# First mixer: the last two pooled projections and two modulation slices come ahead of the last gate projection

## What is computed

```python
u = h @ w_in                                   # 768 x 3072
a = u[..., :CONV_W] * jax.nn.sigmoid(u[..., CONV_W:2 * CONV_W])
bp = u[..., 2 * CONV_W:]
a = dwconv(a, w_dw, b_dw, pad)                 # 31 taps, each channel by itself
a = jax.nn.silu(layernorm(a, ln_g, ln_b))
pooled = jnp.stack([centred_mean(bp[..., g, :], w) - bp[..., g, :]
                    for g, w in enumerate(POOL_WINDOWS)], axis=-2)
p = jnp.einsum('...gc,gcd->...gd', pooled, w_pool) + b_pool
return jnp.concatenate([a, p], axis=-1) @ w_out
...
mod_lat = jnp.split((sc @ w_ada[l] + b_ada[l])[:, None, :], 6, axis=-1)
```

## Time and profile before

| what | value |
|---|---|
| median of three runs | 2460.28 us |
| the profiled execution | 2461.31 us, span 2459.7 us |
| TensorE matmuls busy | 2321.2 us, 94% of the span |
| VectorE busy | 1625.6 us, 66% |
| ScalarE busy | 946.8 us, 38% |
| GpSimd busy | 427.6 us, 17% |
| share of TensorE in the chain that ended last | 81% (DMA 9%, VectorE 4%) |
| mean DMA rate | 264 GB/s |

### The profile page before, as it was taken

One profiled execution on the slowest core, in us unless ns is written; L12 is line 12 of the kernel. 1 busy time (PEld: TensorE's weight loads), 2 busy tenths in 40 slices (PEclk: granted clock), 3 DMA queues, 4 the chain that ended last, 5 costly groups with the idle time before them and its releaser, 6 DMA issues.

```text
span 2459.7 us, 42712 instructions
## 1 busy us (share of the span) xinstructions
PE 2321.2 (94%) x16387; PEld 1553.2 (63%) x16388; DVE 1625.6 (66%) x2005; ACT 946.8 (38%) x1167; POOL 427.6 (17%) x461
## 2 busy tenths in 40 slices
PE   6999989999999999999969999999999899999984
PEld 3555534457888888888847887666644455555542
DVE  2899985447898889888976651677534633454544
ACT  3000014115777777777754232466421111111111
POOL 0633431220000000000020000211000223233323
PEclk8999989999999999999989999999999899999997
DMA  9111075539999999999992132212543979999997
GB/s 342 58 44 59 34 293 167 182 113 402 421 401 388 380 395 383 385 389 392 378 380 81 62 124 104 87 54 75 193 154 140 412 313 376 404 421 420 420 420 309
DMA packets 154320, 649.12 MB, mean 264 GB/s; under 512 B 27866, under 2 KB 42874, under 8 KB 99458
## 3 DMA queue, kind: packets, MB, share of 16 engines
q1 hardware_dynamic: 126624, 577.40, 59.7%
q0 software_dynamic: 16192, 57.53, 6.5%
q10 hardware_dynamic: 11426, 13.12, 1.5%
HBM read 595.13 MB, written 52.86 MB: 263 GB/s over the span
## 4 chain that ended last, share of the span: by engine, by line
PE 81%; DMA 9%; DVE 4%; ACT 2%; issue 2%; POOL 1%; SPq 0%; ACTq 0%; DVEq 0%; POOLq 0%
PE ps L970 78%; DMA arena<-in_w_dram 6%; DMA chunk<-in_w_ada_dram 1%; ACT arena L1616 1%; DVE arena L2380 1%; PE ps L1212 1%; PE ps L1190 1%; PE ps L1196 1%; DMA arena<-h_d,uix 1%; PE ps L1059 1%; POOL arena L769 0%; DMA buf_d<-arena 0%; PE ps L1586 0%; DMA arena<-in_w_ada_dram 0%; DMA arena<-buf_d,slots 0%
## 5 line engine op out<-in xcount | busy, mean ns | idle before, releaser
L970 PE MATMUL ps<-arena 128*32 128x256 f32 (+5 forms) x10296 | 1188.7, 407 | 38.9 <-DVE arena L2380 12.3
L970 PEld LDWEIGHTS ps<-arena 128*32 128x32 f32 (+1 forms) x10296 | 652.5, 129 | 521.1 <-issue 318.5
L2433 DVE TENSOR_TENSOR wl<-wx,wh 128x2048 fp32r<-128x2048 f32 x228 | 511.1, 2285 | 18.5 <-ACT wh L1616 18.5
L1616 ACT ACTIVATE arena<-ps 128x256 f32<-128x256 f32 (+5 forms) x389 | 176.4, 478 | 864.0 <-PE ps L970 616.9
L1616 ACT ACTIVATE wh<-wx 128x2048 fp32r<-128x2048 f32 x228 | 432.4, 1915 | 80.8 <-PE ps L970 75.9
L2380 DVE COPY arena<-arena 128x2048 f32<-128x2048 f32 x180 | 222.7, 1297 | 273.1 <-PE ps L970 228.8
L970 PE MATMUL ps<-wh,xT 128*128 128x512 f32 x1184 | 379.2, 394 | 1.2 <-issue 0.7
L970 PEld LDWEIGHTS ps<-wh,xT 128*128 128x128 f32 x1184 | 222.5, 188 | 53.1 <-issue 1.2
L2502 DVE SCALAR_TENSOR_TENSOR arena<-arena,par 128x768 f32<-128x768 f32 x232 | 241.1, 1112 | 0.0
L970 PE MATMUL ps<-wl,xT 128*128 128x512 f32 x608 | 239.4, 394 | 0.0
L970 PE MATMUL ps<-wh,gT 128*128 128x512 f32 x608 | 199.5, 399 | 0.0
(11 more groups left out here) (362 smaller groups left out, 2267.1 us busy)
## 6 DMA issues: line engine op xcount, KB each, us to landing
wx<-in_w_dram SPq DMA_DIRECT2D x228, 1024.0 KB, 8.4
arena<-in_w_dram SPq DMA_DIRECT2D x192, 1024.0 KB, 21.8
arena<-in_w_ada_dram SPq DMA_DIRECT2D x40, 1024.0 KB, 8.6
craw<-in_w_in_c_dram SPq DMA_DIRECT2D x8, 2048.0 KB, 8.7
buf_d<-arena POOLq DMA_DIRECT2D x1, 14848.0 KB, 57.5
arena<-buf_d POOLq DMA_DIRECT2D x19, 512.0 KB, 10.0
buf_d<-arena POOLq DMA_DIRECT2D x19, 512.0 KB, 7.7
arena<-in_w_in_ab_dram SPq DMA_DIRECT2D x8, 1024.0 KB, 12.6
```

What stands on the lines that cost most here:

```text
L970: return pe.matmul(bank_ap, lhsT, rhs, start=first, stop=last)
L1616: return act.activation(out_, in_, f, **kw)
L2433: v.tensor_tensor(wl[:, g], wx[:, g], whs[g % NH].bitcast(F32), ALU.subtract).then_inc(m["low"], 1)
```

## The change

Only the table of steps is written in another order; loads, buffers, waits inside the steps and all arithmetic stay.

```diff
-for _step in ("V0 G0 P0 V1 G1 P1 V2 G2 P2 V3 p0 G3 P3 V4 p1 G4 P4 V5 G5 P5 V6 p2 G6 p3 V7 P6 G7 p4 P7 "
-              "s0 s1 p5 s2 s3 s4 s5 s6 p6 s7 s8 s9 p7 s10 s11").split():
+for _step in ("V0 G0 P0 V1 G1 P1 V2 G2 P2 V3 p0 G3 P3 V4 p1 G4 P4 V5 G5 P5 V6 p2 G6 p3 P6 V7 P7 s0 s1 G7 "
+              "p4 s2 s3 s4 s5 p5 p6 s6 s7 s8 p7 s9 s10 s11").split():
```

## The result

The changed kernel takes 2464.54 us, the median of 20 runs; the kernel before takes 2460.66 us, the median of 20 runs beside it. The medians lie 3.9 us apart. The ratio is 1.0019 with a 95% interval of 1.0012 to 1.0027, that is 4.7 us (3.0 to 6.6). So the changed kernel is slower: a small loss, by either figure inside the 0.2% that had been called no change, though the upper end of the interval is not. Two of its 20 runs stand apart, 2486.80 and 3494.04 us, at mean granted clocks of 0.95 and 0.63 where the others have 0.97; the second is left out of the ratio, and without both the median is 2464.50 us. The time lies 0.8 us above the predicted 2463.7, and 0.4 of these because the kernel before takes 2460.66 us in the 20 runs and not 2460.28. The profiled execution took 2462.43 us.

The account below looks back on a forecast made before the run. The end of s11 was taken to bound the stage, VectorE next. 2461.31 + 3.4 = 2464.7 us for an execution like the profiled one, which lies 1.03 above the median, so 2463.7 us predicted; range 2459.0 to 2468.5.

Parts of the forecast that it names:

- The limit: End of the stage: set by the end of s11, at 348.43 us before, with VectorE 1.73 us behind as next limit.
- The late gate: G7 ends 13.4 us later, at 310.7; VectorE takes tile 7's product at 322.63, hidden with 11 us to spare.
- The longer wait: SyncE waits for all gates until 310.7, not 297.28; both panels go together, s4 starts at 326.5, TensorE idles 11 us.
- `s4` and `s5`: Slices 4 and 5 on TensorE after the idle: the same 4.45 us as before, ending at 331.0.
- `p5` and `p6`: Projections now ahead of s6: full speed, 2.85 us each; s6 ends at 338.8, 10 us later.
- The wait for GpSimd: TensorE's 3.20 us wait ahead of p6 for GpSimd's tile 7: gone.
- The tail: Loads of s9 to s11, released behind s6 to s8: three left instead of two, s11 ends at 351.8, 3.4 us later.
- VectorE: Convolutions beside GpSimd's pooling: end moves by 0 to 4.2 us, to 361.1 at most, covered by second sums at 362.0.
- Cold projections: Rival: p5 and p6 at half clock, 5.46 us each; +6.0 us with one, +8.6 with both; chance 0.29.
- The full queue: Rival: loads overlap, transfers bound, s11 ends at 346.8; 2458.7 us, or up to 2461.3 with partial overlap; chance 0.15.

Follow-up runs that it names:

- extra load: The changed kernel with one more transfer of 1.25 MB, used by nobody, ahead of the first panel: 2467.95 us.
- panel behind: The changed kernel with SyncE issuing the P-step panel behind P7, then s4's load, and only the gate panel after the wait for G7: 2460.52 us.
- its version with fill: The changed kernel with SyncE's panels reordered, plus six output-projection filler steps instead of four ahead of the wait for the last convolution: 2457.86 us.
- release sooner: The changed kernel with slice n loaded when slice n-4 is done, not n-3, using a fourth load semaphore: 2459.76 us.
- Each half of the change alone: Two kernels: the changed order up to G7 and p4 with the old rest, 2460.41 us; the old order up to s1 with the new rest, 2459.55 us.

## Why the prediction was right

*The limit* was the end of `s11`, and VectorE next: shown from both sides, by the extra load (one to one to the end) and by the panel behind (TensorE at once waits for VectorE).

Times in this section are set on the axis of the kernel before, 1.28 us later than in the rows above. *The late gate* ended at 311.4 for the forecast 310.7, and hid behind VectorE, which took its sigmoid 15 us later. *The longer wait*: the panels left together, `s4` started at 327.3 for 326.5, idle 11.52 for 11. *`s4` and `s5`* took 4.0 us, up to the start of `p5`, instead of 4.45. *`p5` and `p6`* ran at full speed, 2.85 us each, with 1.08 us between them. *The wait for GpSimd* is gone.

*The tail* is the term that was off in size: from the release of `s9` to the end of `s11` I had 13.0 us (338.8 to 351.8); it took 11.6 (339.2 to 350.8), mainly because the three loads landed 2.5 to 2.6 us apart and not 3.4 and 3.2. The 3.4 came from one pair of transfers; the 2.7 us per MB of the same prediction would have been nearer. So `s11` ended 2.3 us later than 348.43, not 3.4. Another 0.6 us, which the sum did not have, was lost in the first sums and their filler, partly at the lower clock. Before they read:

```profile
349.09 2.53 PE L970 MATMUL ps<-arena,ones 128*32 128x512 f32 x16 [0.69 <-ACT arena L1616]
351.55 7.13 PE L970 MATMUL ps<-arena 128*128 128x512 f32 x16
```

Now it is 2.79 and 7.45 us (358.62 less 349.09 is 9.53; here it is 10.10). Together 2.90 us in the profiled execution. The medians say 3.9, with a lower end of 3.0; what fills the difference between one profiled execution and the medians stays open. That 3.4 lies so near the 3.9 is thus partly luck: the tail was 1.1 us too dear, the clock in the first sums was left out, and another part has no account.

*VectorE* ended 0.61 us later, within the 0 to 4.2 allowed for. The 4.2 rest on counts in which a tap cut by the edge of a stretch counts whole, and are a little high: the 29 taps of tile 6 took 30.80 us beside pooling in the kernel before, against 27.03 for those of tile 0, so 3.8 us for one tile of pooling.

*The rivals.* Cold projections did not occur in the profiled execution. They do occur: up to `p5` panel behind and its version with fill run the same program, and `p5` took 4.83 us in the one and 3.41 in the other, with granted clocks of 0.50 and 0.61 in the stretch from 322 to 326 us and of 0.72 and 1.00 in the next 4 us. This is the difference between runs that the Trainium skill (TensorE: Matmul & The Clock Gate, What's actually happening) speaks of; how often it strikes the changed kernel was not measured. The full queue did not come about, since `s9` to `s11` were not issued before `s6`, `s7` and `s8` were done; release sooner, where each slice may go out one step earlier, ends `s11` at 348.2 on this axis, between the 346.8 of this rival and the 350.8 measured.

One thing the prediction did not see: it told the loss as one sum, but it is an interplay. Each half of the change alone costs nothing (92.21 and 91.61 us from `p3` to the second sums, for 92.29; the end of `s11` moves by 0.9 later and 1.3 sooner); only the late queue and the late releases together cost 2.9 us.

## What to carry to other kernels

A step that is moved on one engine also moves every wait of the engine that issues loads: here one gate, 14 us later, held 4 MB and eight more loads behind it, though a later gate cost its own consumer nothing. When work is reordered to remove one wait, the loads that hang on the reordered steps have to be reordered with it; with that done alone (panel behind) the same order came out even with the kernel before, and with the sooner releases and the filler moved ahead as well the whole was 5 us faster than before. And a wait is only worth what the next limit leaves: look for that one first, and for work that can fill the time until it.

## What was not expected

GpSimd's first instruction on a tile can be held up for as long as VectorE's taps go on, or not at all. In the kernel before it took 9.0 us on tile 7, over some ten of VectorE's instructions of about 0.93 us. In the changed kernel it was held on tile 6, and on tile 7, begun in the midst of the taps as well, it was not (start, us, three instructions together):

```profile
277.88 9.59 POOL L769 TENSOR_TENSOR arena<-arena 128x256 f32<-128x256 f32 x3 [14.71 <-ACT arena L1616]
...
298.54 2.95 POOL L769 TENSOR_TENSOR arena<-arena 128x256 f32<-128x256 f32 x3 [2.43 <-ACT arena L1616]
```

What decides between the two was not tried. The Trainium skill (SBUF — State Buffer, Who interferes with whom) says that a VectorE instruction with two inputs in SBUF contends with a GpSimd instruction that reads SBUF. The trace agrees where GpSimd was held, with 9.0 us for one instruction; it was held there for longer than any single instruction of VectorE's lasted.
